# Another order on TensorE around the state inputs, the memory's values and the gated scores

## The chip, the cores and the metric

The kernel runs on one core of a Trainium2 chip. The metric is the device time of one execution in microseconds (us). Three runs of the kernel before took 1558.75, 1558.55 and 1563.71 us, a median of 1558.75. The profiled execution took 1558.66 us.

## The reference

Two transformer blocks run one after the other on 256 tokens of width 1024, in float32. The first block mixes three branches (attention, a convolution, a state space model), then attends to 256 memory tokens, then has a feed-forward layer. The second block mixes an mLSTM and a gated linear attention (GLA), both in two directions, and ends in a layer of 16384 experts. Cut to the parts that the change touches:

```
# block 1: p = h @ w_in, with h = rms_norm(x)
v = p[..., 1024:1536]                            # values of the attention
a, b = split(p[..., 1536:2048])                  # the convolution's input
conv_in = a * sigmoid(b)                         # then 31 taps, a layer norm, silu, a projection
u = p[..., 2048:]                                # the state space model's input
bu = einsum(u, fr * b_re - fi * b_im), einsum(u, fr * b_im + fi * b_re)   # the state inputs
x_t = a_t * x_(t-1) + bu_t                       # a scan over the tokens
y = einsum(x_re, c_re) - einsum(x_im, c_im) + d * u
z = q @ k.T / 8                                  # per head, 8 heads; the stick breaking attention
w = exp(log_sigmoid(z) + later);  o = w @ v
xv = m @ xa_wv                                   # values of the 256 memory tokens
# block 2, per head of 4 and per direction of 2
num = (q @ k.T * decay) @ v;  den = sum(q @ k.T * decay)     # mLSTM
h = num / max(abs(den), floor)
att = (q * exp(b - ref)) @ (k * exp(ref - b)).T  # GLA, per chunk of 64
s_loc = (k * exp(b_end - b)).T @ v               # what each chunk adds to the GLA's state
```

## The kernel before

One program holds the whole computation. Tokens lie along the free axis (256), features on the 128 partitions, so activations are 128x256 tiles, 8 of them for the width. Each engine has its own program, written out by hand in order, and works through it strictly in that order; the engines meet through semaphores.

TensorE writes each product into one of 8 banks of PSUM. They form two rings of four, lower and upper. `begin(key, taker)` takes the next bank of its ring and waits until the engine that takes the product which lay in this bank before (VectorE, `dve`, or ScalarE, `act`) has taken it. `ahead_of(n)` gives the bank n places ahead, with the same wait, without taking it yet. So the order on TensorE also decides which product follows which in a bank. `made` counts the finished products; the other engines wait for the number of the product that they want. Weights come through a ring of six slots in SBUF, loaded by SyncE's queue in the order in which TensorE uses them.

Place 1 is the start of block 1. TensorE projects `u`, `conv_b`, sums the memory's squares (`mem_sum`), projects `conv_a` (L617), transposes the state inputs' table (`b_t`, L618 to L624), makes the 8 state inputs `bu` (L627 to L632; matmuls on 32 partitions each) and the values `v` (L634, L635), then the four `qk` projections. VectorE in the meantime works out the table, takes `u` (L1512), finishes the angles (L1516), takes `conv_a` (L1520), scales the memory's tokens (L1508) and goes through the 62 taps of the convolution (L1533), the rotations of the states (L1542 to L1547), their scans (L1558), the rotations back (L1561 to L1566), a reciprocal (L1570), and L1573, which takes `ssm_y`. L1588 takes the products that scale the queries and keys, and the scores `z` need that. ScalarE copies the table, the state inputs and the values out of PSUM (L2308).

Place 2 is the attention of block 1. `scores`, `later` and `weighted` belong to one head or pair; between them TensorE works on the memory, here `mem_values`, whose weights ScalarE has to round first (L2399) and VectorE has to split (L1625).

Place 3 is the mixing of block 2. `values(hd)` are the products of the mLSTM of a head, `gla_scores` the gated scores of the GLA, then come four sums `add` with a projection (`mo`, `mo`, `gr`, `gr`) behind each. VectorE makes the keys and queries of the gated scores (L1957 to L1959), the low parts of the weight halves (L1807), and the quotients of each head (L1994 to L2005), which take the products of `values`. ScalarE copies the gated scores (L2672) and makes the high parts of the weight halves (L2570). On VectorE the parts of halves 22 and 23 stand ahead of the quotients of the last head; on ScalarE the copies of the gated scores stand ahead of the high parts of the same halves.

Of the kernel before, what the change touches and what calls it, by code (L numbers as in the profile page):

```python
# [16 lines left out]
KD = D // P  # L17
T = 256
TB = T // P
# [10 lines left out]
NS = 8  # L30
# [85 lines left out]
def program(nc, d):  # L116

    plan = Products()
# [4 lines left out]
    with ExitStack() as ctx:  # L123
# [297 lines left out]
        def _(pe):  # L421
            open_items = []

            def after(key, taker=None):
                for r in ([taker] if taker else plan.takers[key]):
                    pe.wait_ge(drained[r], plan.rank[key, r])

            def begin(key, *takers, upper=0):

                before = plan.add(key, takers, upper=upper)  # L430
                if before is not None:
                    after(before)
                return ps[:, plan.bank[key], :]

            def weights(name, i, width=SLOT):

                n = len(items)
                items.append((name, i, width))
                released.append(None)
                open_items.append(n)  # L440
                pe.wait_ge(in_ring[n % RING], landed(n))
                return ring[:, n % RING, 0:width]
# [13 lines left out]
            def release_half(*ns):  # L456

                for n in ns:
                    halves_released[n] = plan.count
# [21 lines left out]
            def project(key, takers, name, i, rhs, nk=KD, halves=2, n=T, upper=0):  # L481

                bank = begin(key, *takers, upper=upper)
                w = weights(name, i, halves * nk * P).rearrange("p (m k c) -> p m k c", m=halves, k=nk)
                for m in range(halves):
                    for k in range(nk):
                        last = mm(bank[:, m * n:(m + 1) * n], w[:, m, k, :], rhs(k), k == 0, k == nk - 1)
                last.then_inc(made, 1)
                release()
# [8 lines left out]
            def tokens(key, takers, w, act, block_, upper=0):  # L498

                bank = begin(key, *takers, upper=upper)  # L500
                for k in range(KD):
                    last = mm(bank, act[:, k, block_ * P:(block_ + 1) * P], w[k // 4][:, k % 4, :], k == 0, k == KD - 1)
                last.then_inc(made, 1)
# [110 lines left out]
            project("conv_b", ("act",), "w_in", 7, arriving("h_mix"))  # L614
            pe.wait_ge(flag("squares_ready"), 1)
            total("mem_sum", [sq[:, k, :] for k in range(KD)])
            project("conv_a", ("dve",), "w_in", 6, hk)  # L617
            pe.wait_ge(flag("constants_ready"), 6)  # L618
            pe.wait_ge(flag("b_ready"), 1)
            bank = begin("b_t", "act")  # L620
            for i in range(4):
                last = nc.tensor.transpose(bank[:, i * P:(i + 1) * P],
                                           bb[:, i // 2, i % 2, :, :].rearrange("p c h -> p (c h)"), ident[:, :])
            last.then_inc(made, 1)  # L624
            after("b_t")
            after("u")
            for c in range(NS):  # L627
                bank = begin(("bu", c), "act")
                rows = slice(32 * (c % 4), 32 * (c % 4) + 32)
                for i in range(2):  # L630
                    last = mm(bank[:, i * T:(i + 1) * T], bb_t[rows, i, c // 4, :], u[rows, c // 4, :])
                last.then_inc(made, 1)  # L632
            wv = [weights("w_in_v", i).rearrange("p (k n) -> p k n", k=4) for i in range(2)]
            for b in range(TB):  # L634
                tokens(("v", b), ("act",), wv, h, b)  # L635
            release()

            def conv_mean():
# [19 lines left out]
            def mem_values(n, b):  # L658

                if b == 0:  # L660
                    mem_wv[:] = [first_weights("xa_wv", 2 * n + i) for i in range(2)]
                    held[:] = open_items
                    open_items.clear()
                bank = begin(("xv", n, b), "act")
                at = slice(b * P, (b + 1) * P)
                for t, (act, which) in enumerate(((memory_high, 1), (memory_low, 1), (memory_high, 2))):
                    for k in range(KD):
                        if b == 0 and k % 4 == 0 and t != 1:
                            pe.wait_ge(first_high_ready if t == 0 else first_split, mem_wv[k // 4][0] + 1)
                        w = mem_wv[k // 4][which].rearrange("p (k n) -> p k n", k=4)  # L670
                        last = mm(bank, act[:, k, at], w[:, k % 4, :], t == 0 and k == 0, t == 2 and k == KD - 1)
                last.then_inc(made, 1)
                if b == TB - 1:
                    for w in mem_wv:
                        first_made[w[0]] = plan.count
                    for i in held:
                        released[i] = plan.count
# [55 lines left out]
            def scores(hd):  # L733
                for i in range(4) if hd >= 4 else (0, 2):
                    after(("qk_r", i))
                rows = slice(64 * (hd % 2), 64 * (hd % 2) + 64)
                bank = begin(("z", hd), "dve")
                mm(bank[:, 0:T], qk[rows, 4 + hd // 2, 0:P], qk[rows, hd // 2, :])
                mm(bank[:, T:T + P], qk[rows, 4 + hd // 2, P:T], qk[rows, hd // 2, P:T]).then_inc(made, 1)
# [10 lines left out]
            def weighted(pair):  # L750
                bank = begin(("o", pair), "act")
                for hd in (2 * pair, 2 * pair + 1):
                    pe.wait_ge(flag("sb_weights_ready"), hd + 1)
                    out = bank[64 * (hd % 2):64 * (hd % 2) + 64, :]
                    w = z_w[:, hd % 4, :]
                    vh = slice(SB_D * hd, SB_D * hd + SB_D)
                    mm(out[:, 0:T], v_sb[:, 0, vh], w[:, 0:T], True, False)
                    last = mm(out[:, P:T], v_sb[:, 1, vh], w[:, T:T + P], False, True)
                last.then_inc(made, 1)
# [31 lines left out]
            scores(4)  # L791
            scores(5)
            weighted(0)
            mem_values(0, 0)
            scores(6)
            scores(7)
            weighted(1)
            mod_items(2)
            later(4)
# [282 lines left out]
            gla_keys()  # L1082
            values_of("gv", 3, wv, 1)
            release_half(*wv)
            gla_scores()
            values(3)

            def mix2_sum(i, squares_):

# [1204 lines left out]
        def _(act):  # L2294
# [11 lines left out]
            def copy_out(key, dst, src=None, scale=1.0):  # L2306
                bank = s.product(key)
                s.took(key, a_(dst, bank if src is None else src(bank), ACT.Copy, scale=scale))  # L2308
# [42 lines left out]
            a_(cond[:, :, 1], cols("c_ctx"), ACT.Silu).then_inc(flag("cond_ready"), 1)  # L2351
            copy_out("b_t", bb_t.rearrange("p i a s -> p (i a s)"))
            for c in range(NS):
                copy_out(("bu", c), bu[:, :, c, :], halves)
            s.wait("turns_ready", 2)
            for i in range(2):
                t = trig[:, i].rearrange("p c t -> p (c t)")
                a_(t, t, ACT.Sin, scale=TURN).then_inc(flag("trig_ready"), 1)
            for b in range(TB):
                copy_out(("v", b), v_sb[:, b, :])  # L2360
            for i in range(4):
                bank = s.product(("qk", i))
                a_(qk[:, 2 * i:2 * i + 2, :], halves(bank), ACT.Copy)
# [715 lines left out]
```

## Time and profile before

| | |
|---|---|
| median of three runs | 1558.75 us |
| profiled execution: its time, its span | 1558.66 us, 1556.9 us |
| TensorE matmuls busy | 1531.8 us, 98% of the span |
| VectorE busy | 1180.3 us, 76% |
| ScalarE busy | 767.1 us, 49% |
| chain of waits that ended last | TensorE 92%, VectorE 4%, DMA 2%, ScalarE 1% |
| mean granted clock of TensorE | 0.997 of full speed |

The span runs from the first to the last instruction; 1.8 us of the time lie around it. The chain of waits is followed back from the last instruction: at each step to what released it, or to the instruction before it on its engine. A row of a timeline has the start and the duration of a run of instructions of one line, and in brackets how long the engine was idle before it and who released it. The records of a matmul of float32 are two, so `x32` there are 16 matmuls of the program. Their durations overlap: each starts before the one ahead of it has drained.

### The profile page before, as it was taken

How to read it: one execution, taken by the hardware profiler on the slowest of the kernel's cores; microseconds unless marked ns; L12 is line 12 of the kernel's file. 1: busy time of each engine (PE TensorE's matmuls, PEld its weight loads, DVE VectorE, ACT ScalarE, POOL GpSimd, SP SyncE). 2: the span in 40 equal slices, each digit the busy share in tenths (PEclk: the TensorE clock that was granted, in tenths of full speed). 3: DMA queues.
4: the chain of work that ended last, by engine and by line, in shares of the span. 5: the costliest groups of instructions: out<-in, count | busy, mean ns of one | idle time of the engine just before them, and what ended most of it. 6: DMA issues, size and time to landing. Idle time of an engine off the chain costs nothing.

```text
span 1556.9 us, 28174 instructions
## 1 busy us (share of the span) xinstructions
PE 1531.8 (98%) x10460; PEld 1385.4 (89%) x10460; DVE 1180.3 (76%) x2029; ACT 767.1 (49%) x1089; POOL 60.4 (4%) x108
## 2 busy tenths in 40 slices
PE   8999999999999999999999999999999999999997
PEld 6678897999999887989999999999999888888886
DVE  7997645776646968757699999988875777777776
ACT  5237544544435563425444654544545545545543
POOL 2002000100000034000000000000000000000000
PEclk9999999999999999999999999999999999999999
DMA  7364658455533230516277777555558777777763
GB/s 298 118 242 158 241 228 318 160 190 185 175 128 104 94 109 1 204 55 243 73 231 221 231 225 218 171 168 153 157 156 294 254 243 242 238 241 243 238 202 95
DMA packets 95942, 293.66 MB, mean 189 GB/s; under 512 B 10480, under 2 KB 45424, under 8 KB 82928
## 3 DMA queue, kind: packets, MB, share of 16 engines
q1 hardware_dynamic: 95712, 292.21, 56.3%
q8 instruction: 60, 0.98, 0.3%
q14 instruction: 26, 0.21, 0.0%
q10 hardware_dynamic: 144, 0.26, 0.0%
HBM read 274.60 MB, written 17.83 MB: 188 GB/s over the span
## 4 chain that ended last, share of the span: by engine, by line
PE 92%; DVE 4%; DMA 2%; ACT 1%; issue 0%; SPq 0%; POOL 0%; DVEq 0%; POOLq 0%
PE ps L479 92%; DVE split_ring L2136 1%; DMA ring<-kept_acts 1%; DMA ring<-in_peer_u 1%; DMA ring<-in_w_in 1%; DVE big L1996 0%; DVE big L2184 0%; DVE big L2188 0%; DVE big L2186 0%; DMA ring<-in_w_gv 0%; DMA kept_acts<-par 0%; ACT split_ring L2735 0%; ACT split_hid_high L2719 0%; PE ps L863 0%; DVE x L2284 0%
## 5 line engine op out<-in xcount | busy, mean ns | idle before, releaser
L479 PE MATMUL ps<-split_hh,split_ring 128*128 128x256 f32 (+1 forms) x3632 | 516.0, 291 | 3.1 <-DVE split_ring L2136 2.9
L479 PEld LDWEIGHTS ps<-split_hh,split_ring 128*128 128x128 f32 x3632 | 456.9, 191 | 14.2 <-DVE split_ring L2136 1.9
L479 PE MATMUL ps<-split_ring 128*128 128x512 f32 (+1 forms) x1472 | 370.2, 382 | 3.0 <-DVE split_ring L2136 3.0
L479 PEld LDWEIGHTS ps<-split_ring 128*128 128x128 f32 x1472 | 268.7, 188 | 58.1 <-DVE split_ring L2136 4.9
L2136 DVE TENSOR_TENSOR split_ring<-ring,split_ring 128x1024 fp32r<-128x1024 f32 x196 | 238.6, 1220 | 49.4 <-ACT split_ring L2735 48.0
L2735 ACT ACTIVATE split_ring<-ring 128x1024 fp32r<-128x1024 f32 x128 | 135.1, 1057 | 78.9 <-DMA ring<-in_peer_u 78.5
L2239 DVE TENSOR_TENSOR ring<-ring,big 128x256 f32<-128x256 f32 x128 | 81.4, 637 | 81.5 <-PE ps L479 70.3
L479 PE MATMUL ps<-split_ffn_h,split_ffn_w 128*128 128x256 f32 x1056 | 127.4, 283 | 0.0
L479 PEld LDWEIGHTS ps<-split_ffn_h,split_ffn_w 128*128 128x128 f32 x1056 | 127.0, 192 | 0.1
L2742 ACT ACTIVATE split_ring<-ring 128x1024 fp32r<-128x1024 f32 x68 | 72.2, 1062 | 94.8 <-PE ps L479 81.5
L1741 DVE TENSOR_TENSOR split_ffn_w<-ring,split_ffn_w 128x2048 fp32r<-128x2048 f32 x33 | 75.6, 2291 | 49.8 <-ACT split_ffn_w L2535 49.8
L479 PE MATMUL ps<-split_hid_high,split_ffn_w 128*128 128x258 f32 (+1 forms) x736 | 112.0, 284 | 0.2
L479 PEld LDWEIGHTS ps<-split_hid_high,split_ffn_w 128*128 128x128 f32 x736 | 102.0, 191 | 1.1 <-ACT split_hid_high L2719 1.0
L2742 ACT ACTIVATE split_ring<-hh 128x1024 fp32r<-128x1024 f32 x60 | 63.8, 1064 | 75.1 <-PE ps L479 74.9
L479 PE MATMUL ps<-big 128*128 128x256 f32 (+11 forms) x632 | 82.5, 327 | 3.3 <-ACT big L2308 1.3
L479 PEld LDWEIGHTS ps<-big 128*128 128x128 f32 (+5 forms) x632 | 64.7, 165 | 23.0 <-issue 10.6
L2308 ACT ACTIVATE big<-ps 128x512 f32<-128x512 f32 (+2 forms) x62 | 28.7, 481 | 110.7 <-PE ps L479 91.1
L2535 ACT ACTIVATE split_ffn_w<-ring 128x2048 fp32r<-128x2048 f32 x33 | 63.1, 1912 | 40.1 <-PE ps L479 40.1
L2218 DVE TENSOR_SCALAR ring<-tables,idx 128x128 f32<-128x128 f32 x256 | 71.3, 344 | 5.9 <-PE ps L479 5.9
L2136 DVE TENSOR_TENSOR split_hh<-hh,split_ring 128x1024 fp32r<-128x1024 f32 x60 | 73.1, 1218 | 0.0
L479 PE MATMUL ps<-ring 128*128 128x128 f32 x512 | 62.4, 275 | 0.0
L479 PEld LDWEIGHTS ps<-ring 128*128 128x128 f32 x512 | 60.0, 192 | 0.0
(350 smaller groups left out, 2007.6 us busy)
## 6 DMA issues: line engine op xcount, KB each, us to landing
ring<-in_peer_u SPq DMA_DIRECT2D x128, 512.0 KB, 3.9
ring<-in_peer_v SPq DMA_DIRECT2D x68, 512.0 KB, 3.5
hh<-in_peer_v SPq DMA_DIRECT2D x60, 512.0 KB, 3.5
ring<-in_w_mod SPq DMA_DIRECT2D x24, 1024.0 KB, 5.7
ring<-in_ffn_in SPq DMA_DIRECT2D x22, 1024.0 KB, 4.9
ring<-kept_acts SPq DMA_DIRECT2D x128, 128.0 KB, 3.1
ring<-in_ffn_out SPq DMA_DIRECT2D x11, 1024.0 KB, 4.8
ring<-in_w_out SPq DMA_DIRECT2D x8, 1024.0 KB, 9.2
```

The costliest lines, as they stand in the source:

```text
L479: return nc.tensor.matmul(out, lhsT, rhs, start=start, stop=stop, skip_group_check=True)
L1741: v.tensor_tensor(fw_low[:, q, :], ring[:, (ffn_at + n) % RING, :], fw_high[:, q, :].bitcast(F32), ALU.subtract).then_inc(flag("weights_sp ...
L2136: v.tensor_tensor(low, tile, high.bitcast(F32), ALU.subtract).then_inc(flag(kind + "_split"), 1)
L2218: v.tensor_scalar(hot[n % 4][:, q, 0, :], iota, idx[:, 0, at:at + 1], idx[:, 2, at:at + 1], ALU.is_equal, ALU.mult)
L2239: v.tensor_tensor(weighted_[:, q, :], act_in[:, q, :], g_, ALU.mult).then_inc(flag("whole_weighted"), 1)
L2308: s.took(key, a_(dst, bank if src is None else src(bank), ACT.Copy, scale=scale))
L2535: a_(fw_high[:, n % 3, :], ring[:, at % RING, :], ACT.Copy).then_inc(flag("weights_rounded"), 1)
L2735: a_(u_high[q], u_tile[:, q, :], ACT.Copy).then_inc(flag("u_high_ready"), 1)
L2742: a_(v_high[q % 4], v_tile[q], ACT.Copy).then_inc(flag("v_high_ready"), 1)
```

## The change

At place 1 the projection `conv_a` is cut into its two halves of 8 matmuls, with the transposes of the table between them; the table takes the next bank and `conv_a` the one behind it. The first block of values comes after four of the state inputs. ScalarE copies in the same order. At place 2 the scores of heads 6 and 7 stand ahead of the memory's first values. At place 3 the last `values` stand ahead of the gated scores.

```diff
             total("mem_sum", [sq[:, k, :] for k in range(KD)])
-            project("conv_a", ("dve",), "w_in", 6, hk)
+            conv_bank = ahead_of(1)
+            w = weights("w_in", 6).rearrange("p (m k c) -> p m k c", m=2, k=KD)
+
+            def half_conv(m):
+
+                for k in range(KD):
+                    last = mm(conv_bank[:, m * T:(m + 1) * T], w[:, m, k, :], h[:, k, :], k == 0, k == KD - 1)
+                return last
+
+            half_conv(0)
             pe.wait_ge(flag("constants_ready"), 6)
             pe.wait_ge(flag("b_ready"), 1)
             bank = begin("b_t", "act")
...
             last.then_inc(made, 1)
+            last = half_conv(1)
+            plan.add("conv_a", ("dve",))
+            assert ps[:, plan.bank["conv_a"], :] == conv_bank
+            last.then_inc(made, 1)
+            release()
             after("b_t")
             after("u")
+            wv = [weights("w_in_v", i).rearrange("p (k n) -> p k n", k=4) for i in range(2)]
             for c in range(NS):
+                if c == NS // 2:
+                    tokens(("v", 0), ("act",), wv, h, 0)
                 bank = begin(("bu", c), "act")
...
-            wv = [weights("w_in_v", i).rearrange("p (k n) -> p k n", k=4) for i in range(2)]
-            for b in range(TB):
-                tokens(("v", b), ("act",), wv, h, b)
+            tokens(("v", 1), ("act",), wv, h, 1)
             release()
...
             weighted(0)
-            mem_values(0, 0)
             scores(6)
             scores(7)
+            mem_values(0, 0)
             weighted(1)
...
             release_half(*wv)
+            values(3)
             gla_scores()
-            values(3)
...
             for c in range(NS):
+                if c == NS // 2:
+                    copy_out(("v", 0), v_sb[:, 0, :])
                 copy_out(("bu", c), bu[:, :, c, :], halves)
...
-            for b in range(TB):
-                copy_out(("v", b), v_sb[:, b, :])
+            copy_out(("v", 1), v_sb[:, 1, :])
```

TensorE at place 1, before: the projection `conv_a` (`hh,ring`), the table's transposes (`tables,big`) and the first state inputs (`big`). A `products_taken_by_...` in brackets is the wait for the bank.

```order
L479 MATMUL ps<-hh,ring 128x256 [waits weights_in_slot2,products_taken_by_scalar]
L479 MATMUL ps<-hh,ring 128x256 x15
L622 MATMUL ps<-tables,big 128x128 [waits products_taken_by_vector,b_ready,constants_ready]
L622 MATMUL ps<-tables,big 128x128 x3
L479 MATMUL ps<-big 128x256 [waits products_taken_by_scalar,products_taken_by_vector]
L479 MATMUL ps<-big 128x256
L479 MATMUL ps<-big 128x256 [waits products_taken_by_scalar]
L479 MATMUL ps<-big 128x256
```

The same place now, up to the first block of values (`ring,hh`):

```order
L479 MATMUL ps<-hh,ring 128x256 [waits weights_in_slot2,products_taken_by_vector]
L479 MATMUL ps<-hh,ring 128x256 x7
L631 MATMUL ps<-tables,big 128x128 [waits products_taken_by_scalar,b_ready,constants_ready]
L631 MATMUL ps<-tables,big 128x128 x3
L479 MATMUL ps<-hh,ring 128x256 x8
L479 MATMUL ps<-big 128x256 [waits weights_in_slot4,weights_in_slot3,products_taken_by_scalar,products_taken_by_vector]
L479 MATMUL ps<-big 128x256
L479 MATMUL ps<-big 128x256 [waits products_taken_by_scalar]
L479 MATMUL ps<-big 128x256
L479 MATMUL ps<-big 128x256 [waits products_taken_by_scalar]
L479 MATMUL ps<-big 128x256
L479 MATMUL ps<-big 128x256 [waits products_taken_by_vector]
```

The first wait for a bank has passed from the table to `conv_a`: ScalarE's product lay in the first bank, VectorE's `u` in the second, and the two have changed places.

TensorE at place 2, the change against the kernel before: two scores (two matmuls each, `big`), and the first of the memory's values (`first,split_hh` and `split_ring,split_hh`).

```order
+L479 MATMUL ps<-big 128x256
+L479 MATMUL ps<-big 128x128
+L479 MATMUL ps<-big 128x256
+L479 MATMUL ps<-big 128x128
 L479 MATMUL ps<-first,split_hh 128x512 x16
 L479 MATMUL ps<-split_ring,split_hh 128x512 x8
-L479 MATMUL ps<-big 128x256
-L479 MATMUL ps<-big 128x128
-L479 MATMUL ps<-big 128x256
-L479 MATMUL ps<-big 128x128
```

The four matmuls of the two scores have moved past the 24 of the values.

TensorE at place 3, before: the gated scores (`64x64`), the last values with their sums over ones, and the first sum (`64x128`).

```order
L479 MATMUL ps<-big 64x64 [waits products_taken_by_scalar,gla_ready]
L479 MATMUL ps<-big 64x64 x15
L479 MATMUL ps<-big 64x64 [waits products_taken_by_scalar]
L479 MATMUL ps<-big 64x64 x15
L479 MATMUL ps<-big 128x256 [waits products_taken_by_vector,scores_ready]
L479 MATMUL ps<-big 128x256 x2
L479 MATMUL ps<-big 128x128
L479 MATMUL ps<-big,ones 128x256 [waits weights_summed]
```

And now:

```order
L479 MATMUL ps<-big 128x256 [waits products_taken_by_vector,scores_ready]
L479 MATMUL ps<-big 128x256 x2
L479 MATMUL ps<-big 128x128
L479 MATMUL ps<-big,ones 128x256 [waits weights_summed]
L479 MATMUL ps<-big 128x256 [waits products_taken_by_vector]
L479 MATMUL ps<-big 128x256 x2
L479 MATMUL ps<-big 128x128
L479 MATMUL ps<-big,ones 128x256 [waits weights_summed]
L479 MATMUL ps<-big 64x64 [waits products_taken_by_scalar,gla_ready]
L479 MATMUL ps<-big 64x64 x15
L479 MATMUL ps<-big 64x64 [waits products_taken_by_scalar]
L479 MATMUL ps<-big 64x64 x15
```

The ten matmuls of the last values now stand ahead of the 32 of the gated scores. Nothing moves on VectorE, GpSimd or SyncE's queue.

## Rows read from the trace of the kernel before

**Rows 1.** TensorE's timeline: start us, duration us, what, [idle before <- who released it].

```profile
25.20 3.62 PE L479 MATMUL ps<-big,ones 128*128 128x256 f32 x16
28.65 7.07 PE L479 MATMUL ps<-hh,ring 128*128 128x256 f32 x32
35.55 0.60 PE L622 MATMUL ps<-tables,big 128*128 128x128 f32 x4
36.84 1.20 PE L479 MATMUL ps<-big 32*128 32x256 f32 x16 [0.69 <-ACT big L2308]
38.65 3.54 PE L479 MATMUL ps<-big 32*128 32x256 f32 x16 [0.61 <-ACT big L2308]
42.12 16.18 PE L479 MATMUL ps<-ring,hh 128*128 128x512 f32 x32
...
106.92 1.96 PE L479 MATMUL ps<-big 128*32 128x256 f32 x32
...
114.72 2.25 PE L479 MATMUL ps<-big 64*128 64x256 f32 x16 [0.38 <-DVE big L1588]
```

**Rows 2.** Windows: stretch, its length, busy of PE, PEld, DVE, ACT, POOL; clock, DMA.

```profile
38.00:40.00 2.00, 1.39 (x10) 1.29 (x10) 1.97 (x5) 2.00 (x5) 0.00 (x0) 0.93 0.91 385
40.00:42.00 2.00, 2.00 (x10) 1.32 (x7) 2.00 (x6) 1.48 (x4) 0.00 (x0) 0.50 0.00 0
...
46.00:50.00 4.00, 4.00 (x10) 1.57 (x10) 4.00 (x11) 0.42 (x1) 0.00 (x0) 0.93 0.00 0
```

**Rows 3.** VectorE's timeline in the first 110 us.

```profile
31.15 0.69 DVE L1512 TENSOR_TENSOR big<-ps,big 128x512 f32<-128x512 f32 x1
...
36.16 0.68 DVE L1520 TENSOR_TENSOR big<-ps,big 128x512 f32<-128x512 f32 x1
...
104.53 3.35 DVE L1570 RECIPROCAL big<-big 128x512 f32<-128x512 f32 x1
108.95 1.00 DVE L1573 SCALAR_TENSOR_TENSOR big<-big,par,ps 128x256 f32<-128x256 f32 x2 [1.06 <-PE ps L479]
```

**Rows 4.** All waits of VectorE from 30 to 115 us: sum us, times, longest.

```profile
DVE big L1573 <- PE ps L479: 1.1, 1, 1.1
```

**Rows 5.** TensorE's timeline at place 2.

```profile
142.30 3.01 PE L479 MATMUL ps<-first,split_hh 128*128 128x512 f32 x12 [0.97 <-ACT first L2399]
...
147.06 1.74 PE L479 MATMUL ps<-big 64*128 64x256 f32 x16
```

**Rows 6.** ScalarE's timeline at place 2.

```profile
140.35 1.90 ACT L2399 ACTIVATE first<-ring 128x2048 fp32r<-128x2048 f32 x1
```

**Rows 7.** TensorE's timeline at place 3.

```profile
622.94 4.40 PE L479 MATMUL ps<-big 64*64 64x64 f32 x72 [0.92 <-DVE big L1959]
625.55 1.78 PE L479 MATMUL ps<-big 128*128 128x256 f32 x8
...
629.65 1.59 PE L479 MATMUL ps<-big 64*64 64x128 f32 x32
...
637.11 1.59 PE L479 MATMUL ps<-big 64*64 64x128 f32 x32
```

**Rows 8.** ScalarE's timeline at place 3.

```profile
624.57 2.41 ACT L2672 ACTIVATE big<-ps 64x512 f32<-64x512 f32 x4 [1.92 <-PE ps L479]
627.01 2.01 ACT L2570 ACTIVATE split_ring<-ring 128x1024 fp32r<-128x1024 f32 x2
```

**Rows 9.** VectorE's timeline at place 3.

```profile
628.10 2.41 DVE L1807 TENSOR_TENSOR split_ring<-ring,split_ring 128x1024 fp32r<-128x1024 f32 x2 [4.08 <-ACT split_ring L2570]
630.43 0.41 DVE L1994 SCALAR_TENSOR_TENSOR big<-ps,big 128x256 f32<-128x256 f32 x1
...
636.28 0.42 DVE L2002 TENSOR_TENSOR big<-ps,big 128x256 f32<-128x256 f32 x1
```

**Rows 10.** TensorE's first matmuls by tile: duration ns min/median/max, starts in us.

```profile
L479 PE MATMUL ps<-big,ones x7: 584/631/763, 5.9 to 8.6; 128*128 128x256 f32 x7
...
L479 PE MATMUL ps<-big,ones x10: 379/379/584, 8.6 to 10.7; 128*128 128x256 f32 x10
```

## The prediction

> **What bounds the kernel now.** I read the page first: TensorE is busy for 98% of the span and is 92% of the chain that ended last, so the time is almost everywhere what TensorE's own instructions take, and a change of order can gain only where TensorE waits or runs slowly. The timeline of TensorE shows those places. Around the state inputs it waits 0.69 and 0.61 us for ScalarE's copies, and the second half of the state inputs takes 3.54 us where the first took 1.20 [rows 1]. The windows then show its only half-clock stretch before the end: the granted clock is 0.93 on average over 38 to 40 us, 0.50 after that and 0.93 over 46 to 50, so it is at 1.2 GHz instead of 2.4 from about 39.7 to 46.6 us [rows 2]. The values' matmuls start inside it, at 42.12 [rows 1]. At 142.30 it waits 0.97 us for ScalarE's rounding [rows 5, 6], and at 622.94 it waits 0.92 us for VectorE's L1959 [rows 7]. These are the three places the change touches.
>
> The timeline of VectorE is the second thing to read, and it says something the page doesn't. Between 30 and 115 us VectorE waits once in all, 1.06 us before L1573 at 108.95 [rows 3, 4]. So from 31.15, where it takes the product `u`, up to 108.95 it is a second chain, only 1.06 us shorter than TensorE's. From 108.95 the chain that ended last runs over VectorE to the scores at 114.72. What makes VectorE late by more than 1.06 us in this stretch makes the whole kernel late; what makes TensorE early gains at most that 1.06.
>
> **Place 1: the table inside the convolution's projection.** No instruction is added or taken away; the cost is in which bank each product gets. Before, `conv_a` had the bank of `mix_sum`, which ScalarE had long emptied. Now the table takes that bank, and `conv_a` gets the one of `u`. VectorE empties `u` with L1512, at 31.15 + 0.69 = 31.84 [rows 3]. TensorE comes there at 25.20 + 3.62 = 28.82 [rows 1]. So the first half of `conv_a` must wait 3.1 us, and nothing else is queued in between that could fill it: TensorE runs in program order and every instruction behind it waits too. This is the step on which my forecast rests.
>
> Then: start at 31.9; the projection takes 7.07 and the table 0.45 to 0.60 in its middle [rows 1]; I take 0.45, since the tail of 0.60 lies beside the next matmul. `conv_a` is complete at 31.9 + 7.07 + 0.45 = 39.4 instead of 35.7. VectorE wants it at 36.16 (L1520) and had no wait there [rows 3]; now it starts at 39.5, 3.3 us late. Behind L1520 stand the convolution's 62 taps and the rotations of the states, all on VectorE and without a wait [rows 4], so everything up to the reciprocal at 104.53 comes 3.3 us later. That reciprocal then ends at 104.53 + 3.35 + 3.3 = 111.2, and L1573 follows at 111.2 instead of 108.95: the 1.06 us of slack are used up and **2.3 us** are left over [rows 3]. TensorE waits for what follows L1573, so the scores move from 114.72 to 117.0 [rows 1].
>
> What place 1 gains on TensorE lies under this. Both waits of 0.69 and 0.61 are covered or shortened, four state inputs are copied out beside the first 8 values' matmuls, and if the clock stays up, the values take 2.2 us less than their 16.18 [rows 1], half of what lies between 42.12 and 46.6 [rows 2]. From 28.82 to the end of the values I count 3.1 for the wait, 7.35 for projection and table, 1.8 and 1.4 for the state inputs with their copies and 13.8 for the values, so the next projection starts at 56.1 to 56.3 instead of 58.1, even with the new wait. But these 2.0 us are given back before `ssm_y`: TensorE is there at 104.9 instead of 106.92 [rows 1] and waits for the states until 104.5 + 3.3 = 107.8. Bounds of place 1: if VectorE were not delayed, -1.06; with the wait for `u` and a clock that falls after it, 2.3 plus what is below under the clock rival. I take +2.3, since each of its rows is there and none is an estimate of something unseen. ScalarE's copies and its sine of the angles move too, and cost nothing: VectorE wants both only after the taps.
>
> **Place 2: two scores before the memory's values.** The two scores fill the wait of 0.97 at 142.30 [rows 5]. The wait itself ends when ScalarE's rounding ends, at 140.35 + 1.90 = 142.25 [rows 6], and that doesn't move. 147.06 shows two scores and a weighted sum in 1.74 us; half of it is 0.87, less than the 0.97. So what is saved is the **0.87 us** of the two scores after the values. For it VectorE must have emptied the banks of scores 4 and 5, which it does while score 6 runs. The bounds: -0.97 (the whole wait) and 0 (the banks are late by as much). I take -0.9.
>
> **Place 3: the last values before the gated scores.** The wait of 0.92 goes, as the last values need nothing of L1959. They take 629.65 - 625.55 = 4.1 us and the gated scores 625.55 - 622.94 = 2.61 [rows 7]. New order: values 622.02 to 626.12, gated scores to 628.73, first sums 0.92 early. But ScalarE's copy of the gated scores starts 1.63 us after them (624.57 against 622.94), so it moves to 626.12 + 1.63 = 627.75, 3.2 us later [rows 7, 8]. Behind it on ScalarE stand the high parts of two weight halves (627.01), and VectorE has its own part of these halves ahead of the quotients of the last head: it waits for them until 628.10 and starts the quotients at 630.43 [rows 8, 9]. All of it moves by 3.2. The last product of the values is taken at 636.28 + 0.42 + 3.2 = 639.9 [rows 9]. Its bank is the one of the second group of the second sum, which TensorE would want 0.8 us after 637.11 - 0.92 = 636.2 [rows 7]. So it waits at 637 to 639.9, and the sum ends at 639.93 + 0.8 = 640.7 instead of 637.11 + 1.59 = 638.7: **+2.0 us**. After that VectorE has caught up (its next halves are wanted only 3 us later), and nothing more is lost. The bounds are -0.92, if VectorE isn't late, and +2.0. The value is again the one that the rows give.
>
> **Sum.** 2.3 - 0.9 + 2.0 = +3.4 us. The profiled execution took 1558.66 us, a span of 1556.9 and 1.8 around it, within 0.1 of the median of 1558.75. Forecast: 1558.7 + 3.4 = 1562.1, 0.2% slower.
>
> **The rivals.**
> *The clock falls after a new wait.* Place 1 makes TensorE idle for 3.1 us after 28.8, and again for about 2.9 before `ssm_y`; place 3 makes it idle for 2.4. In this trace the clock fell after waits of 0.69 and 0.61 between narrow matmuls, and stayed up through the 0.97 and the 0.92, so longer waits put it at risk. What it costs: at the start of the program it ran cold, a 128x256 record mostly in 631 ns from 5.9 to about 9 us, against 379 after that [rows 10], so a half-clock stretch beside dense work costs about half of 3.1, 1.6 us; the one at 39.7 to 46.6 would cost half of 6.9, 3.4. Only the one after 28.8 (it delays `conv_a`) and the one at 637 come through in full. That gives 1563.7 to 1567, 1565 in the middle. The Trainium skill (TensorE: Matmul & The Clock Gate, Part 1, "HAM oscillation") warns of just this: idle gaps between bursts of matmuls bring the clock back to half, and where its monitor stands differs from run to run. The trace agrees on the place (the fall at 39.7 comes after the two waits of 0.69 and 0.61); that it differs from run to run no run here shows yet.
> *TensorE sets the time all along (faster).* VectorE's slack is larger than I read, say because it takes `u` as soon as it is there or the late `conv_a` is made up for among the taps; and the quotients aren't in the way at place 3. Then the 1.06 of place 1, 0.9 and 0.9 come as gains: 1558.7 - 2.9 = 1555.8. If the first stretch were bound by TensorE alone it would be 2.0 + 0.9 + 0.9, 1554.9. For it speaks the page, with 92% of the chain on TensorE. Against it, VectorE's rows with no wait between 31 and 108. It decides whether VectorE starts L1520 later than 36.16 + 1.06 = 37.2.
> *Place 3 keeps its gain.* Place 1 is as I say, but the second sum isn't held up: 2.3 - 0.9 - 0.9 = +0.5, 1559.2. For it: VectorE's work can only be as late as ScalarE's copies, whose 3.2 us are worked out over two engines.
>
> **How the numbers follow.** My forecast without a further fall of the clock 0.50, with it 0.22, place 3 with its gain 0.13, faster 0.09, another thing 0.06. The time is that of the likeliest, 1562.1. The range leaves out the fastest case and the worst of the clock: 1557.5 to 1566.0. What a measurement of this kernel can tell from no change is about 0.5%, 7.8 us. No case but several falls of the clock together reaches 1566.5, and none 1550.9. So faster 0.02, same 0.91, slower 0.07.
>
> **What the profile of the changed kernel will show.** Place 1: TensorE idle some 3 us before the first 16 records of `conv_a`, released by VectorE's L1512; VectorE idle over 3 us before L1520 and no longer idle before L1573; TensorE idle before `ssm_y`; scores at about 117. Place 2: no wait, or below 0.2 us, at the memory's values. Place 3: no wait before the values; a wait of over 2 us before the second sum, released by L2002. I am wrong if L1520 starts before 37.2, if the scores start before 115, or if the second sum has no wait.

## The result, and the profile after

The changed kernel is slower, by about twice what I forecast. Fifteen of its sixteen executions took 1563.67 to 1569.94 us and one took 3065.13; the median of all sixteen is 1566.57 us, and of the fifteen, which alone are in the ratio, 1566.45. The kernel before, timed again beside it, took 1559.51 us (16 executions). The ratio is 1.0042, 95% interval 1.0034 to 1.0050, which is +6.5 us (the medians are 7.1 apart) where I had written +3.4, and the median lies outside my range, which ended at 1566.0. The profiled execution took 1565.65 us with a span of 1563.9, 7.0 more than the span before.

Two lines of the page: busy times, and the chain that ended last.

```profile
PE 1533.0 (98%) x10460; PEld 1386.8 (89%) x10460; DVE 1180.4 (75%) x2029; ACT 765.3 (49%) x1089; POOL 60.6 (4%) x108
...
PE 86%; DVE 9%; DMA 3%; ACT 1%; issue 1%; SPq 0%; DVEq 0%; POOL 0%; POOLq 0%; ACTq 0%
```

Nobody has more to do: TensorE is busy 1533.0 us against 1531.8. But VectorE's share of the chain went from 4% to 9%. 5% of the span is 78 us, about the stretch from its take of `conv_a` at 41.46 to the end of its reciprocal at 113.18 (72 us), over which the chain now runs on VectorE.

TensorE's timeline at place 1, to be laid beside [rows 1]:

```profile
24.93 3.62 PE L479 MATMUL ps<-big,ones 128*128 128x256 f32 x16
32.06 5.41 PE L479 MATMUL ps<-hh,ring 128*128 128x256 f32 x16 [3.51 <-DVE big L1527]
37.30 0.60 PE L631 MATMUL ps<-tables,big 128*128 128x128 f32 x4
37.74 3.62 PE L479 MATMUL ps<-hh,ring 128*128 128x256 f32 x16
41.29 2.05 PE L479 MATMUL ps<-big 32*128 32x256 f32 x16
43.27 7.13 PE L479 MATMUL ps<-ring,hh 128*128 128x512 f32 x16
...
109.85 1.98 PE L479 MATMUL ps<-big 128*32 128x256 f32 x32 [1.78 <-DVE big L1581]
...
118.77 2.25 PE L479 MATMUL ps<-big 64*128 64x256 f32 x16 [0.86 <-DVE big L1603]
```

`conv_a` waits 3.51 us for VectorE's take of `u` (L1527, the L1512 of before), and then its two halves, which are the same 16 records each, take 5.41 and 3.62 us. A difference of 1.79 between equal work is the clock, and the windows say so (columns as in [rows 2]):

```profile
32.00:34.00 2.00, 1.94 (x7) 1.71 (x8) 2.00 (x2) 0.00 (x0) 0.00 (x0) 0.81 0.00 0
34.00:36.00 2.00, 2.00 (x6) 1.57 (x5) 2.00 (x2) 0.00 (x0) 0.00 (x0) 0.50 0.00 0
36.00:38.00 2.00, 2.00 (x11) 1.67 (x11) 0.40 (x1) 0.06 (x1) 0.00 (x0) 0.83 0.00 0
...
644.00:646.00 2.00, 2.00 (x13) 2.00 (x12) 1.97 (x3) 0.17 (x1) 0.00 (x0) 0.56 0.00 0
646.00:648.00 2.00, 2.00 (x12) 2.00 (x12) 1.89 (x5) 0.00 (x0) 0.00 (x0) 0.59 0.00 0
```

The granted clock is at half, 1.2 GHz, for about 3.4 us behind the new wait, and again for about 3.4 us at place 3. The stretch of 39.7 to 46.6 us [rows 2] is gone: the values' first 16 records take 7.13 us, and there is no wait among the state inputs.

VectorE's timeline at place 1, which answers to [rows 3]:

```profile
31.31 0.69 DVE L1527 TENSOR_TENSOR big<-ps,big 128x512 f32<-128x512 f32 x1
...
41.46 0.69 DVE L1535 TENSOR_TENSOR big<-ps,big 128x512 f32<-128x512 f32 x1 [5.06 <-PE ps L479]
...
109.83 3.35 DVE L1585 RECIPROCAL big<-big 128x512 f32<-128x512 f32 x1
113.10 0.90 DVE L1588 SCALAR_TENSOR_TENSOR big<-big,par,ps 128x256 f32<-128x256 f32 x2
```

and all of VectorE's waits from 30 to 116 us, which answer to [rows 4]:

```profile
DVE big L1535 <- PE ps L479: 5.1, 1, 5.1
```

The one wait of VectorE in this stretch stood before L1573; now it stands before the take of `conv_a` (L1535, before L1520) and L1588, the L1573 of before, has none. That looks like the forecast, the slack used up; but the three other profiled executions of the order of before, among the experiments, had none to use up.

Place 2 on TensorE, which answers to [rows 5]: no wait before the memory's values.

```profile
142.21 2.94 PE L479 MATMUL ps<-big 128*128 128x128 f32 x26
145.22 4.14 PE L479 MATMUL ps<-first,split_hh 128*128 128x512 f32 x16
```

Place 3 on TensorE, which answers to [rows 7]:

```profile
624.86 1.68 PE L479 MATMUL ps<-big 128*128 128x256 f32 x8
...
628.86 4.06 PE L479 MATMUL ps<-big 64*64 64x64 f32 x96
...
639.61 1.09 PE L479 MATMUL ps<-big 64*64 64x128 f32 x16 [0.74 <-ACT big L2696]
642.68 1.09 PE L479 MATMUL ps<-big 64*64 64x128 f32 x16 [1.98 <-DVE big L2017]
643.70 3.35 PE L479 MATMUL ps<-split_head,split_ring 128*128 128x256 f32 x16
...
651.12 1.59 PE L479 MATMUL ps<-big 64*64 64x128 f32 x32
```

ScalarE, which answers to [rows 8]:

```profile
630.49 2.42 ACT L2688 ACTIVATE big<-ps 64x512 f32<-64x512 f32 x4 [4.83 <-PE ps L479]
632.93 2.01 ACT L2586 ACTIVATE split_ring<-ring 128x1024 fp32r<-128x1024 f32 x2
```

VectorE, which answers to [rows 9]:

```profile
634.02 2.41 DVE L1822 TENSOR_TENSOR split_ring<-ring,split_ring 128x1024 fp32r<-128x1024 f32 x2 [6.98 <-ACT split_ring L2586]
636.35 0.41 DVE L2009 SCALAR_TENSOR_TENSOR big<-ps,big 128x256 f32<-128x256 f32 x1
...
642.20 0.42 DVE L2017 TENSOR_TENSOR big<-ps,big 128x256 f32<-128x256 f32 x1
```

The wait before the values is gone. ScalarE's copies start 1.63 us behind the gated scores (630.49 against 628.86), the same as before, then come the roundings, then VectorE, and the second group of the second sum starts 0.06 us after VectorE's L2017 ends at 642.62. Its first group waits 0.74 us too. The profile names ScalarE's L2696 for that, which ends at 639.50; I take it to be VectorE's L2013, which ends at 639.46. By the ring of four, the first group gets the bank of the product that L2013 takes, and in a run below with ScalarE's work in another order this sum starts before ScalarE's copy does.

To add up, I cut the span at four marks that every version has: VectorE's take of `u`, the scores, the product over ones that ScalarE releases at 165.24 before (168.44 after), and at place 3 the last record ahead of the moved work (621.63; 624.64) and the third sum (644.57; 651.12).

| us | before | after | difference | forecast |
|---|---|---|---|---|
| start to the take of `u` | 31.15 | 31.31 | +0.16 | 0 |
| place 1: take of `u` to the scores | 83.57 | 87.46 | +3.89 | +2.3 |
| place 2: scores to the product over ones | 50.52 | 49.67 | -0.85 | -0.9 |
| from there to place 3 | 456.39 | 456.20 | -0.19 | 0 |
| place 3 | 22.94 | 26.48 | +3.54 | +2.0 |
| third sum to the end of the span | 912.33 | 912.78 | +0.45 | 0 |
| span | 1556.9 | 1563.9 | +7.0 | +3.4 |

Two places are too dear, by 1.6 and 1.5 us, and each has a stretch at half clock in it. The 83.57 of before has one in it as well [rows 2].

### The profile page after: what moved, and what is told of

The parts are those of the page before. It is cut to its first block, busy times and chain, and to the rows that moved or that the text cites. A ratio compares the mean times of both kernels' runs of the same rounds, so it can differ in the third digit from the quotient of the medians.

```text
span 1563.9 us, 28174 instructions
## 1 busy us (share of the span) xinstructions
PE 1533.0 (98%) x10460; PEld 1386.8 (89%) x10460; DVE 1180.4 (75%) x2029; ACT 765.3 (49%) x1089; POOL 60.6 (4%) x108
## 4 chain that ended last, share of the span: by engine, by line
PE 86%; DVE 9%; DMA 3%; ACT 1%; issue 1%; SPq 0%; DVEq 0%; POOL 0%; POOLq 0%; ACTq 0%
PE ps L479 85%; DVE big L1548 1%; DVE split_ring L2151 1%; DMA ring<-kept_acts 1%; DMA ring<-in_peer_u 1%; DVE big L1573 1%; DVE big L2011 0%; DMA ring<-in_peer_v 0%; DVE big L1455 0%; DVE big L2199 0%; DVE big L2203 0%; DVE big L2201 0%; DMA ring<-in_w_gv 0%; DMA x<-in_x 0%; DMA kept_acts<-par 0%
## 5 line engine op out<-in xcount | busy, mean ns | idle before, releaser
L479 PE MATMUL ps<-hh,ring 128*128 128x256 f32 x256 | 58.3, 388 | 3.5 <-DVE big L1527 3.5
```

What stands on the lines that cost most here:

```text
L479: return nc.tensor.matmul(out, lhsT, rhs, start=start, stop=stop, skip_group_check=True)
```

## The experiments

Each row below is one version, timed beside the kernel before (11 executions of each version, but 16 of the changed kernel, 7 of place 1 alone and 5 of place 1 filled). The columns for the places are from its one profiled execution, us between the same marks; the last says at which place its clock was at half (tail: near 1540 us), TensorE's idle end left out.

| version | median, before beside it | ratio (95%) | place 1 | place 2 | place 3 | half clock at |
|---|---|---|---|---|---|---|
| after | 1566.57, 1559.51 | 1.0042 (1.0034 to 1.0050) | 87.46 | 49.67 | 26.48 | 1, 3 |
| banks alone | 1562.51, 1559.55 | 1.0021 (1.0012 to 1.0030) | 87.17 | 50.54 | 22.92 | 1 twice |
| place 1 alone | 1563.63, 1559.55 | 1.0029 (1.0018 to 1.0040) | 88.58 | 50.55 | 22.96 | 1, tail |
| place 1 filled (too long) | 1568.11, 1559.55 | 1.0043 (1.0029 to 1.0057) | 89.04 | 49.66 | 27.88 | 3 |
| place 3 alone | 1563.26, 1559.55 | 1.0023 (1.0014 to 1.0032) | 82.30 | 50.56 | 27.84 | 3 |
| both waits filled | 1563.15, 1559.52 | 1.0025 (1.0016 to 1.0034) | 85.99 | 49.65 | 25.16 | tail |
| banks back | 1562.12, 1559.52 | 1.0016 (1.0006 to 1.0025) | 82.35 | 49.71 | 26.50 | 3, tail |
| place 3 mended, alone | 1556.71, 1559.52 | 0.9984 (0.9975 to 0.9993) | 82.31 | 50.54 | 21.63 | 1 |
| whole change, both mended | 1556.08, 1559.52 | 0.9977 (0.9968 to 0.9986) | 82.33 | 49.70 | 21.62 | none |
| places 2 and 3 mended | 1556.07, 1559.62 | 0.9978 (0.9969 to 0.9987) | 82.30 | 49.67 | 21.62 | none |
| place 1 mended, alone | 1559.73, 1559.62 | 1.0002 (0.9992 to 1.0011) | 82.33 | 50.59 | 22.97 | none |

**Only the banks.** The order of before, but `conv_a` goes into the bank of `u` and the table into that of `mix_sum`.

```diff
-            project("conv_a", ("dve",), "w_in", 6, hk)
+            bank = ahead_of(1)
...
+                    last = mm(bank[:, m * T:(m + 1) * T], w[:, m, k, :], h[:, k, :], k == 0, k == KD - 1)
+            plan.add("conv_a", ("dve",))
...
-            bank = begin("b_t", "act")
+            after("mix_sum")
+            bank = ps[:, 0, :]
```

> The kernel before in its old order; only the banks of conv_a and of the table change places, so conv_a waits for VectorE to take u. Theory 1 (the bank): TensorE idle 3 to 3.5 us before conv_a, L1520's counterpart starts at 39.0 without a fall of the clock and at 40.7 with one, scores start at 116.5 or 118.2 instead of 114.7; time +1.8 to +3.5 us. Rival (the new order of table, state inputs and values costs the time, not the bank): scores start at 114.7, time unchanged.

TensorE's timeline of it:

```profile
31.50 8.86 PE L479 MATMUL ps<-hh,ring 128*128 128x256 f32 x32 [3.43 <-DVE big L1523]
```

The wait is there with nothing moved, and the projection takes 8.86 us where it took 7.07 [rows 1]. Exchanging two banks costs 3.0 us of the median (1562.51 against 1559.55), its falls of the clock included, and the scores start at 117.92. So the bank is enough to make place 1 dear; the runs with the banks back, below, show that the order costs nothing.

**Place 1 alone.** The first two parts of the diff and ScalarE's, without places 2 and 3.

> Place 1 of the change alone. Theory 1: the wait for u and a half-clock stretch behind it put the scores at 118.8 as in the changed kernel, time +4.0 us (2.3 of the wait, 1.7 of the clock). Rival (place 3 costs more than it seems and place 1 costs only the 2.3 of the wait): +2.3 us.

```profile
32.69 6.53 PE L479 MATMUL ps<-hh,ring 128*128 128x256 f32 x16 [3.50 <-DVE big L1527]
```

The same wait (3.50), and half clock for the whole of the first half: 6.53 us against 5.41 in the changed kernel. The clock is at half for 6.8 us here and for 3.4 there, though everything up to this point is the same code. The median is 4.1 us above that of before.

**The wait of place 1 filled.** The changed kernel with products into a free bank, which nobody reads, ahead of `conv_a`.

```diff
             total("mem_sum", [sq[:, k, :] for k in range(KD)])
+            for n in range(14):
+                mm(ps[:, 4, 0:T], ones, sq[:, n % KD, :])
             conv_bank = ahead_of(1)
```

> The changed kernel with 14 matmuls of 128x256, whose results nobody reads, in the wait before conv_a, so that TensorE isn't idle; conv_a can't start earlier than before. Clock theory: no half-clock stretch from 33 to 37 us, conv_a is out at 39.5 instead of 41.4, scores start at 117.0 instead of 118.8, time 1.7 us below the changed kernel. Rival (the matmuls of conv_a are slow for another reason, say the VectorE's and the queue's reads beside them): they stay slow, scores at 118.8, time as the changed kernel.

```profile
25.82 9.66 PE L479 MATMUL ps<-big,ones 128*128 128x256 f32 x44
35.31 3.62 PE L479 MATMUL ps<-hh,ring 128*128 128x256 f32 x16
```

I had sized it wrongly: 14 products are 28 records, 6.1 us, about twice the wait. So `conv_a` starts at 35.31, 3.4 us after VectorE has taken `u` (31.89), and the time (1568.11, two of five executions 1564.4) says nothing on what the clock costs. What the rows do say: with TensorE kept busy the clock stays up, and the first half takes 3.62.

**Place 3 alone.**

```diff
             release_half(*wv)
-            gla_scores()
             values(3)
+            gla_scores()
```

> Place 3 of the change alone. Theory 2 (the copies of the gated scores push the rounding of halves 22 and 23, that pushes VectorE's quotients, and they hold the bank of the second sum): no wait before the values, a wait of 2 to 2.4 us inside the second sum released by L2002, +2.0 us and up to 1.6 more if the clock falls after it: +2.0 to +3.6. Rival (place 3 gains its 0.9 us when place 1 doesn't disturb the clock ahead of it): -0.9.

TensorE's timeline, and its windows:

```profile
635.82 1.09 PE L479 MATMUL ps<-big 64*64 64x128 f32 x16 [0.74 <-ACT big L2680]
638.89 1.97 PE L479 MATMUL ps<-big 64*64 64x128 f32 x16 [1.98 <-DVE big L2002]
```

```profile
640.00:642.00 2.00, 2.00 (x15) 1.67 (x12) 1.97 (x3) 0.38 (x1) 0.00 (x0) 0.50 0.00 0
```

The same two waits of 0.74 and 1.98, then half clock over 6.8 us: 27.84 us to the third sum instead of 22.94. Swapping these two calls costs 3.7 us of the median; the wait of 0.92 that it takes away is not to be seen in the time.

**Both waits filled**, now each to its size.

```diff
             total("mem_sum", [sq[:, k, :] for k in range(KD)])
+            for n in range(7):
+                mm(ps[:, 4, 0:T], ones, sq[:, n, :])
             conv_bank = ahead_of(1)
...
                 for odd in ((1, 0) if i < 2 else (0, 1)):
+                    if (i, odd) == (1, 0):
+                        for n in range(9):
+                            mm(ps[:, 6, 0:P], ones, ones)
```

> The changed kernel with matmuls whose results nobody reads in its two longest waits: 7 of 128x256 (14 records, 3.0 us) before conv_a, 9 of 128x128 (18 records, 1.9 us) inside the second sum of place 3. They can't start conv_a or the sum earlier, they only keep TensorE working. Clock theory: no half-clock stretch at either place, scores at 117.0, the second sum and what follows only 2.0 us late; time 1.7 + 1.5 us below the changed kernel, some 1563 against 1566.6. Rival (the clock falls with or without the waits, or the slow matmuls are slow for another reason): time as the changed kernel.

TensorE's timeline of it:

```profile
25.15 6.64 PE L479 MATMUL ps<-big,ones 128*128 128x256 f32 x30
31.63 3.62 PE L479 MATMUL ps<-hh,ring 128*128 128x256 f32 x16
...
638.39 2.27 PE L479 MATMUL ps<-ones 128*128 128x128 f32 x18
640.60 1.09 PE L479 MATMUL ps<-big 64*64 64x128 f32 x16
641.62 2.18 PE L479 MATMUL ps<-split_head,split_ring 128*128 128x256 f32 x16
...
647.56 1.59 PE L479 MATMUL ps<-big 64*64 64x128 f32 x32
```

This is the experiment that settles the size. `conv_a` and the second group of the second sum still start only after VectorE has let them, 0.38 and 0.22 us behind its takes (0.06 in the changed kernel, so the filling is 0.3 and 0.2 us too long); only TensorE's idling in the two longest waits is gone. The 0.74 us ahead of the second sum are still there, and alone they don't bring the clock down. The clock stays up at both places (2.18 us for the 16 records that took 3.35), place 1 takes 85.99 and place 3 25.16, and the median is 1563.15 instead of 1566.57; ten of its eleven executions took 1561.40 to 1563.79, where the fastest of the changed kernel took 1563.67. More work on TensorE makes the kernel 3.4 us faster. Against before, 3.6 us are left, some 0.5 of them the filling's, where my sum was 3.4.

**The banks back.** The whole change, but `conv_a` keeps the bank of `mix_sum` and the table goes into that of `u`.

```diff
-            conv_bank = ahead_of(1)
+            conv_bank = ahead_of(0)
...
-            bank = begin("b_t", "act")
+            bank = ahead_of(1)
+            plan.add("b_t", ("act",))
...
             plan.add("conv_a", ("dve",))
+            plan.bank["b_t"], plan.bank["conv_a"] = plan.bank["conv_a"], plan.bank["b_t"]
+            plan.in_bank[plan.bank["b_t"]], plan.in_bank[plan.bank["conv_a"]] = "b_t", "conv_a"
```

> The whole change, but conv_a keeps the bank of mix_sum and the table that of u. Theory 1: no wait before conv_a, which is out at 36.2; VectorE takes it at 36.3; no fall of the clock; scores start at 114.0 to 114.2, bound by VectorE; TensorE waits for the states at about 105; with -0.85 of place 2 and +3.6 of place 3 the time is +2.0 to +2.7 us against the kernel before. Rival (cutting conv_a in two and the values among the state inputs cost something of their own): +4 us or more.

```profile
33.24 0.63 PE L632 MATMUL ps<-tables,big 128*128 128x128 f32 x4 [0.15 <-DVE big L1530]
...
114.75 2.25 PE L479 MATMUL ps<-big 64*128 64x256 f32 x16 [0.86 <-DVE big L1606]
```

Half of `conv_a` now covers the wait for `u`: 0.15 us are left of 3.51, no half clock, 82.35 at place 1. What remains, +2.6 us, is about place 3 less place 2 (+3.56 and -0.81 between the marks).

**Place 3 with ScalarE's order turned round as well.** On ScalarE the high parts of halves 22 and 23 go ahead of the copies of the gated scores, so VectorE no longer hangs on the gated scores.

```diff
-            gla_scores()
             values(3)
+            gla_scores()
...
             copy_out(("gv", 3), gv[:, 3, :])
+            half_high(22, 23)
             s.wait("att_zeroed")
...
-            half_high(22, 23)
```

> Place 3 alone as in e4, and on ScalarE the rounding of halves 22 and 23 ahead of the copies of the gated scores. Theory 2: VectorE's quotients start at most 0.5 us later than in the kernel before, no wait inside the second sum, no fall of the clock, the 0.9 us are gained: -0.9 us, scores of e4 taken away. Rival (the rounding waits for its DMA and holds up the gated scores' copies and with them the GLA's outputs; or the wait is due to the bank order alone): +1 to +3.6 us.

ScalarE's timeline, and TensorE's:

```profile
626.59 1.06 ACT L2570 ACTIVATE split_ring<-ring 128x1024 fp32r<-128x1024 f32 x1 [0.20 <-DMA ring<-in_w_mo]
627.55 2.40 ACT L2673 ACTIVATE big<-ps 64x512 f32<-64x512 f32 x4
...
635.30 0.60 ACT L2680 ACTIVATE big<-ps 128x512 f32<-128x512 f32 x1 [4.05 <-PE ps L479]
```

```profile
635.20 1.59 PE L479 MATMUL ps<-big 64*64 64x128 f32 x32
```

The second sum has no wait at all, place 3 takes 21.63 us, 1.31 less than before, and the kernel is faster than the one before: -2.8 us, where I had expected -0.9. Place 3 explains 1.3 of that; no trace shows the other 1.5. In the same order on TensorE that cost 3.7 us in the run above, one line moved on ScalarE is worth 6.5. The sum at 635.20 starts before ScalarE's L2680 at 635.30, which is why I don't believe the name in the bracket of 0.74 us above.

**Both mends with the whole change.** The diffs of the last two runs together.

> The whole change with the banks of e6 and ScalarE's order of e7. If all three places then gain what TensorE saves: place 1 -0.7 (VectorE's chain sets the end there), place 2 -0.85, place 3 -0.9, together -2.4 us against the kernel before, 1557.1. Rival (the gains don't add, since each moves a later wait): -1 or less.

1556.08 us, and 82.33, 49.70 and 21.62 in the three columns. That beats the kernel before by 3.4 us (I had expected 2.4) and the changed one by 10.5.

**What mended place 1 is worth in it.** Two versions: the one with both mends less all of place 1 (its lines as before), and place 1 with its banks back by itself (places 2 and 3 as before).

> The kernel before with place 2 (the two scores ahead of the last values) and place 3 with ScalarE's rounding of halves 22 and 23 ahead of the copies of the gated scores; place 1 is left in the order of before. Places add up: the version with place 3 so mended alone took 1556.7 and place 2 is worth 0.85 in the spans, so 1555.9 if nothing is gained at place 1; the whole change with both mends took 1556.1. Theory 1 (place 1 with its banks back is worth nothing by itself, VectorE sets the end there): this run is within 0.5 of 1556.1, and the scores start 82.3 after VectorE's take of u. Rival (mended place 1 is worth something because TensorE no longer idles and its clock doesn't fall between 40 and 47): this run is 1557 or more, and it has that stretch at half clock while the scores start as late as before.

> Place 1 alone, with conv_a in the bank that mix_sum gives it and the table in the bank that it had before. Theory 1 (VectorE sets the end there): no wait of 3 us ahead of conv_a, scores 82.3 after VectorE's take of u against 83.6 in the profile before, time within 1 us of before. Rival (the order itself costs): slower by 1 us or more, scores later than 84 after the take of u.

1556.07 without place 1 and 1556.08 with it; 1559.73 for place 1 alone against 1559.62. Nothing of it is to be seen in the time: in both VectorE releases the scores after a wait of 0.86 us, 82.3 us after its take of `u`, as in the run above with the banks back. TensorE's scores with place 1 mended alone:

```profile
113.62 2.25 PE L479 MATMUL ps<-big 64*128 64x256 f32 x16 [0.86 <-DVE big L1606]
```

The rival, a gain from the half-clock stretch that mended place 1 doesn't have, finds nothing for it in the medians, though the interval (down to 0.9992) leaves room for 1.2 us. Places 2 and 3 are 2.2 us shorter between the marks, and the median falls by 3.6: as with place 3 mended alone, some 1.4 us of the gain stand in no trace.

## Why the prediction was wrong

By its own steps:

*Place 1, +2.3.* Right as a mechanism: the bank, the wait for L1512, its length (3.51 for 3.1), VectorE's one wait now before L1520. In the run with both waits filled VectorE takes `conv_a` 3.67 us later behind `u` than before, 0.3 of it the filling's, where I had 3.3. Against the profiled execution of before the size is right too: 85.99 - 83.57 = 2.4 us.

One term of it was an accident of that execution: the slack of 1.06 us. The 83.57 has the half-clock stretch of [rows 2] in it, which made TensorE late and so gave VectorE its wait. In the three other profiled executions of the order of before (place 3 alone, place 3 mended alone, places 2 and 3 mended) VectorE waits nowhere from 30 us to the scores, and place 1 takes 82.30 us. The row of the 1.06 us in the first of them:

```profile
108.36 0.90 DVE L1573 SCALAR_TENSOR_TENSOR big<-big,par,ps 128x256 f32<-128x256 f32 x2
```

Against these, place 1 with its wait filled costs 3.7 us and not 2.4: nothing of VectorE's delay is absorbed. Which of the two an execution of before usually is, isn't settled. The medians with both waits filled (+3.6) and with both mends (-3.4) fit 83.57, those with the banks back (+2.6) and with place 1 mended alone (+0.1) fit 82.30.

*Place 2, -0.9.* -0.85 in the changed kernel, and -0.8 to -0.9 in every version that has it.

*Place 3, +2.0.* Right in its chain, from the copies 1.63 us behind the gated scores to the bank that L2002 releases (642.62; my 639.9 and the 3.0 us by which this place comes later make 642.9). The one wait that I forecast is two, 0.74 and 1.98. With the clock kept up it is 25.16 - 22.94 = 2.2, 0.2 of it the filling's.

*The clock: the step that failed.* I gave the fall after a new wait 0.22 and forecast the time without it. It fell behind the new wait of place 1 in all three profiled versions that have it unfilled, and behind that of place 3 in all four; where either wait was filled (two versions, one version) or mended (three versions each), it did not fall there. The fall was the rule, not the exception. I had 1.6 us for one, from [rows 10]. In the changed kernel the two cost 1.5 and 1.3 us by the difference to the filled version, 1.8 and 1.5 without the filling's excess; the stretches of 6.8 us in other versions cost up to 2.6 (place 1) and 2.7 (place 3), less than the 3.4 that I had for such a length. The middle of that case, 1565, is nearer the truth than my forecast. What misled me is that I weighed [rows 5] and [rows 7], where the clock stayed up through 0.97 and 0.92 us, against one fall after 0.69 and 0.61, though the new waits of 3.51 and 1.98 us are about three and a half and two times as long as the longest of these.

The Trainium skill (TensorE: Matmul & The Clock Gate, Part 1, "HAM oscillation") says that idle gaps between dense bursts bring the clock to half. At place 1 the traces agree, with their 3.5 us. At place 3 the gaps are shorter than those which that section describes, 0.74 and 1.98 us with a sum of 1.09 us of narrow matmuls between them, and the clock fell there too, four times in four.

*The range.* Its upper end, 1566.0, left out "the worst of the clock", which was close to the typical. With the 1.6 and 1.5 us by which the two places came out too dear, the sum is 1558.7 + 3.4 + 1.6 + 1.5 = 1565.2, and the median of before was now 0.8 higher than the one that I started from: 1566.0. The last 0.6 to the median of 1566.57 isn't settled. Of the fifteen executions, the four whose mean granted clock was 0.995 took 1566.16 to 1569.94 us, the profiled one 1565.65 at 0.997, so the longer ones had more of half clock. Where, no trace shows.

## What to carry to other kernels

When products rotate through banks, a change of order on one engine is also a change of who waits for whom: list for each moved product the one that lay in its bank and when that is taken, and for each product taken later what stands behind it on the engine that takes it. Here a mend of a few lines on the other engine, or the two banks exchanged, turned +3.7 us into -2.8 and +4.1 into 0. A new wait of 2 to 3.5 us on a TensorE that is otherwise dense should be priced with the half clock behind it: here it came behind the two new waits in seven cases of seven, though behind an old one of 1.6 to 2.0 us near the end in only three of twelve. Work in its place, even work that nobody reads, cost less than the idling did. And a slack that is read from one profile should be checked for a half-clock stretch ahead of it: it may be there in that execution only.

## What the runs showed that I had not expected

Whether and how long the clock is at half differs between executions of the same instructions. In the order of before at place 1 it was from 39.7 to 46.6 us in one profiled execution, from 42.0 to 45.4 in another, and not at all in two; with only the banks exchanged, where the state inputs follow the same two waits (0.69 and 0.64 us), it was there again for 3.4 us. The windows of the version with place 3 mended alone show the second:

```profile
42.00:44.00 2.00, 2.00 (x4) 0.69 (x3) 1.96 (x7) 2.00 (x2) 0.00 (x0) 0.51 0.00 0
44.00:46.00 2.00, 2.00 (x4) 0.83 (x3) 2.00 (x6) 2.00 (x2) 0.00 (x0) 0.64 0.00 0
```

There is such a place near the end as well, unchanged in all versions, after a wait of 1.6 to 2.0 us for VectorE: in three of the twelve profiled executions the 18 records behind it took about 6.0 us instead of 4.5, as in the version with both waits filled:

```profile
1540.00:1542.00 2.00, 2.00 (x7) 1.57 (x8) 1.32 (x2) 0.00 (x0) 0.00 (x0) 0.72 0.00 0
1542.00:1544.00 2.00, 2.00 (x7) 1.51 (x6) 0.00 (x0) 0.58 (x1) 0.00 (x0) 0.50 0.00 0
```

And the take of `u` starts anywhere between 30.56 and 32.40 us in twelve profiled executions with the same work ahead of it, so a difference of 1 us between two spans needs a mark inside the kernel before it means anything.
